# A convolution moved from VectorE to GpSimd, and 256-column mixing matmuls over two banks, in a two-layer trunk

## What is computed

```
h = RMSNorm(x);  P = h @ W_in
A  = Bg * conv3(C * xa)                      # short causal convolution, 3 taps, 512 channels
Bm = gelu(u) * (tril(W_s) LN(gelu(v)) + b)   # chunks of 128 tokens, 4 groups of 128 channels
Cm = stick-breaking attention                # 8 heads x 64, QK-norm, strictly causal
merged = sum_i sigmoid(gate_i) * (branch_i @ W_branch_out[i])
x = x + merged @ W_o
x = x + SwiGLU(RMSNorm(x)) @ W_down          # d_ff 2816
```

## Time and profile before

| | before |
|---|---|
| median of 3 runs | 1646.74 us |
| the profiled execution | 1646.1 us |
| its span | 1644.4 us |
| TensorE busy | 1636.7 us |
| VectorE busy | 969.1 us |
| ScalarE busy | 783.5 us |
| GpSimd busy | 50.8 us |
| VectorE busy in 60 to 280 us (pairs and first merge of layer 0) | 191.09 of 220 us |

### The profile page before, as it was taken

The page is one execution under the profiler, slowest core; times in us unless marked ns, Lnnn a source line. Parts: engine busy times, 40 slices in busy tenths (PEclk is TensorE's granted clock), DMA queues, the critical chain, the costliest instruction groups (busy, mean ns, idle before and its releaser), DMA issues.

```text
span 1644.4 us, 20945 instructions
## 1 busy us (share of the span) xinstructions
PE 1636.7 (100%) x7394; PEld 1360.2 (83%) x7394; DVE 969.1 (59%) x1302; ACT 783.5 (48%) x1113; POOL 50.8 (3%) x49
## 2 busy tenths in 40 slices
PE   9999999999999999999999999999999999999999
PEld 8888888888888888888888888888888888888887
DVE  6898887554554434434648888875455544344344
ACT  7788886333343223223457888763334432232231
POOL 1000000000120000000120000000001100000000
PEclk9999999999999999999999999999999999999999
DMA  5222222223323223232332222223233232323223
GB/s 195 97 68 78 78 89 72 96 89 102 102 91 101 96 96 101 90 103 89 125 119 90 77 77 77 78 77 98 94 102 102 90 102 90 102 92 99 97 95 128
DMA packets 46860, 158.15 MB, mean 96 GB/s; under 512 B 5456, under 2 KB 5712, under 8 KB 46800
## 3 DMA queue, kind: packets, MB, share of 16 engines
q1 hardware_dynamic: 46656, 157.34, 29.2%
q10 hardware_dynamic: 144, 0.03, 0.0%
HBM read 155.26 MB, written 2.10 MB: 96 GB/s over the span
## 4 chain that ended last, share of the span: by engine, by line
PE 94%; DVE 4%; ACT 1%; DVEq 1%; issue 0%; ACTq 0%
PE bank L461 28%; PE bank L462 28%; PE bank L465 28%; PE z L489 2%; PE z L563 1%; PE bank L489 1%; PE z L462 1%; PE z L465 1%; PE z L461 1%; PE misc L586 1%; PE misc L583 1%; DVE w_lo L1179 1%; PE z L552 1%; PE z L551 1%; DVE S L1348 0%; DVE v_all L1409 0%
## 5 line engine op out<-in xcount | busy, mean ns | idle before, releaser
L461 PE MATMUL bank<-xg_hi,w_hi 128*128 128x512 f32 x1472 | 574.4, 390 | 0.0
L462 PE MATMUL bank<-xg_lo,w_hi 128*128 128x512 f32 x1472 | 573.4, 390 | 0.0
L789 ACT ACTIVATE w_hi<-raw 128x1024 fp32r<-128x1024 f32 (+1 forms) x294 | 302.3, 1034 | 472.2 <-DMA raw<-in_w_units 471.8
L1179 DVE TENSOR_TENSOR w_lo<-raw,w_hi 128x1024 fp32r<-128x1024 f32 (+1 forms) x294 | 357.2, 1219 | 38.7 <-ACT w_hi L789 21.5
L465 PE MATMUL bank<-xg_hi,w_lo 128*128 128x512 f32 x1472 | 364.1, 389 | 0.0
L462 PEld LDWEIGHTS bank<-xg_lo,w_hi 128*128 128x128 f32 x1472 | 276.5, 188 | 56.9
L465 PEld LDWEIGHTS bank<-xg_hi,w_lo 128*128 128x128 f32 x1472 | 276.2, 188 | 57.2
L461 PEld LDWEIGHTS bank<-xg_hi,w_hi 128*128 128x128 f32 x1472 | 276.3, 188 | 56.8
L1184 DVE TENSOR_TENSOR S<-bank,rstd 128x512 f32<-128x512 f32 x152 | 105.0, 691 | 256.1 <-PE bank L465 254.5
L461 PE MATMUL bank<-mid_hi,w_hi 128*128 128x512 f32 x474 | 184.6, 389 | 0.0
L462 PE MATMUL bank<-mid_lo,w_hi 128*128 128x512 f32 x474 | 184.4, 389 | 0.0
(11 more groups left out here) (204 smaller groups left out, 1708.7 us busy)
## 6 DMA issues: line engine op xcount, KB each, us to landing
raw<-in_w_units SPq DMA_DIRECT2D x278, 512.0 KB, 3.3
raw<-in_w_units SPq DMA_DIRECT2D x20, 256.0 KB, 2.6
xT<-in_x SPq DMA_DIRECT2D x8, 256.0 KB, 6.4
out_x<-xT SPq DMA_DIRECT2D x7, 256.0 KB, 4.1
ln_g<-in_sgu_ln_g SPq DMA_DIRECT2D x2, 256.0 KB, 4.9
ln_b<-in_sgu_ln_b SPq DMA_DIRECT2D x2, 256.0 KB, 5.4
sgu_bias<-in_sgu_b SPq DMA_DIRECT2D x2, 256.0 KB, 5.8
sw_raw<-in_sgu_w SPq DMA_DIRECT2D x2, 256.0 KB, 6.0
```

What stands on the lines that cost most here:

```text
L461: mm(dst[:, :], wh[:, k0 + k, :], his[k], start=(k % per == 0), stop=False)
L462: mm(dst[:, :], wh[:, k0 + k, :], los[k], start=False, stop=False)
L789: af(w_hi[at.slot(c)][:, 0:kc, :], raw[at.slot(c)][:, 0:kc, :], ACT.Copy).then_inc(hi_done, 1)
L1179: tt(w[:, 0:kc, :], r[:, 0:kc, :], h[:, 0:kc, :].bitcast(F32), ALU.subtract).then_inc(lo_done, 1)
```

## The change

The five convolution instructions leave VectorE. VectorE now only signals (conv_x), and GpSimd runs the product, three scalings by a tap (tensor_scalar) and three tensor_tensor instructions more, with a drain after each. The second and third tap are a scaling into conv_part and an addition each. Two new semaphores guard the buffers: conv_read (the product has read S1 and S2, waited for before the next unit is written to S2) and mix_read.

The rounded and remainder parts of W_s lie side by side, so one matmul of 256 columns makes hi*hi and hi*lo in two halves; one of 128 columns adds lo*hi to the first half. Chunks 0 and 1 go to misc, 2 and 3 to the bank of unit 8, which unit 4 used before. VectorE adds bias and halves in four instructions of 256 columns.

The order moves: square_lo ahead of attention_lo in all pairs; in pair 0 the last LayerNorm chunk behind the causal mask; unit 4's scaling ahead of fold_sums in all pairs but the last; ya_round on ScalarE behind yb_round and the table load, ya_rest on VectorE behind the next unit 0's scaling; in the last pair the convolution starts ahead of split_lo of unit 6, and ya_round and ya_rest come after gelu_u and with_u.

```diff
+            def convolution(pairs, j):
+                tap = lambda k: par[:, R_CW + 4 * k + j:R_CW + 4 * k + j + 1]
+                pool.wait_ge(conv_x, pairs + 1)
+                nc.gpsimd.tensor_tensor(conv_in[:, 2:2 + T], S1[:, :], S2[:, :], ALU.mult).then_inc(conv_read, 1)
+                pool.drain()
+                nc.gpsimd.tensor_scalar(S1[:, :], conv_in[:, 2:2 + T], tap(2), par[:, R_CB + j:R_CB + j + 1],
+                                        ALU.mult, ALU.add)
+                pool.drain()
+                for k in (1, 0):
+                    nc.gpsimd.tensor_scalar(conv_part[:, :], conv_in[:, k:k + T], tap(k), None, ALU.mult)
+                    pool.drain()
+                    nc.gpsimd.tensor_tensor(S1[:, :], S1[:, :], conv_part[:, :], ALU.add)
+                    pool.drain()
+                nc.gpsimd.tensor_tensor(S1[:, :], S1[:, :], S0[:, :], ALU.mult).then_inc(ya_pre, 1)
                 pool.drain()
...
+                pool.wait_ge(par_in, l * 16 + 16)
+                for j in range(PAIRS):
+                    convolution(l * PAIRS + j, j)
...
-            def mix(n_misc, j, l):
+            def mix(at, n_misc, j, l):
...
+                pe.wait_ge(bank_free[at.slot(8)], at.round(8))
                 for n in range(NT):
-                    cut = slice(n * P, (n + 1) * P)
-                    mm(misc[:, cut], yb_hi[:, j, cut], sw_hi[:, j, :], start=True, stop=False)
-                    mm(misc[:, cut], yb_hi[:, j, cut], sw_lo[:, j, :], start=False, stop=False)
-                    last = mm(misc[:, cut], yb_lo[:, j, cut], sw_hi[:, j, :], start=False, stop=True)
+                    cut, base = slice(n * P, (n + 1) * P), n % 2 * 2 * P
+                    dst = misc if n < 2 else bank[at.slot(8)]
+                    mm(dst[:, base:base + 2 * P], yb_hi[:, j, cut], sw_both[:, j, :, :].rearrange("p a t -> p (a t)"),
+                       start=True, stop=False, skip_group_check=True)
+                    last = mm(dst[:, base:base + P], yb_lo[:, j, cut], sw_hi[:, j, :], start=False, stop=True,
+                              skip_group_check=True)
...
                     scores(h3 + 6, pairs + 1, 0)
+                    pe.wait_ge(mix_read, pairs + 1)
                     unit(pl["A"](j + 1), 0, xh, xl)
...
                     split_hi(at, 10)
                     yb_round()
                     ln_exp_table()
+                    ya_round()
...
+                    square_lo(l * 8 + (j * 2 + 3))
                     attention_lo(h3)
-                    square_lo(l * 8 + (j * 2 + 3))
...
                     yc_add(heads, 0)
+                    scaled(at, 4, S1[:, :])
                     fold_sums(heads + 1)
-                    scaled(at, 4, S1[:, :])
...
+                    convolution()
                     k_rest(heads + 4)
-                    convolution()
-                    mixed(m0 + M_MIX, j1)
+                    mixed(at, m0 + M_MIX, j1)
                     split_lo(at, 9)
+                    dve.wait_ge(conv_read, pairs + 1)
                     scaled(at, 6, S2[:, :])
...
-                    b = sgu_bias[:, j1, :].broadcast_to([P, NT, P])
-                    tt(N0[:, :].rearrange("p (n t) -> p n t", n=NT), misc[:, :].rearrange("p (n t) -> p n t", n=NT),
-                       b, ALU.add).then_inc(misc_free, 1)
+                    for dst, parts in halves:
+                        tt(dst, parts[:, :, 0, :], sgu_bias[:, j1, :].broadcast_to([P, 2, P]), ALU.add)
+                    dve.drain()
+                    tt(halves[0][0], halves[0][0], halves[0][1][:, :, 1, :], ALU.add).then_inc(misc_free, 1)
+                    tt(halves[1][0], halves[1][0], halves[1][1][:, :, 1, :], ALU.add).then_inc(mix_read, 1)
```

More of the change, by code:

```diff
@@ L150, in build @@
         sgu_bias = sb("sgu_bias", [P, KC, P])
-        sw_hi = sb("sw_hi", [P, KC, P], F32R)
-        sw_lo = sb("sw_lo", [P, KC, P], F32R)
+        sw_both = sb("sw_both", [P, KC, 2, P], F32R)
+        sw_hi, sw_lo = sw_both[:, :, 0, :], sw_both[:, :, 1, :]
         yb_hi = sb("yb_hi", [P, KC, T], F32R)
@@ L196, in build @@
         conv_in = sb("conv_in", [P, 2 + T])
+        conv_part = sb("conv_part", [P, T])
         N2 = conv_in[:, 2:2 + T]
@@ L289, in build @@
         yc_ok = sem("yc_ok")
+        conv_x = sem("conv_x")
+        conv_read = sem("conv_read")
         ya_pre = sem("ya_pre")
@@ L301, in build @@
         yb_bank_free = sem("yb_bank_free")
+        mix_read = sem("mix_read")
         silu_in = sem("silu_in")
@@ L1050, in pair @@
                     act.wait_ge(qk_nrm, heads + 4)
+                    if j == 0:
+                        ln_round(l, 3)
                     yc_half(m0 + M_E0)
@@ L1436, in flat @@
                         return t[:, j1, :].rearrange("p a t -> p (a t)")
-                    def tap(k):
-                        return par[:, bass.ds(j + (R_CW + 4 * k), 1)]
                     def convolution():
                         dve.drain()
[L1444 to L1452, removed]
+                        dve.sem_inc(conv_x, 1)
                     def ya_rest():
@@ L1489, in pair @@
                         split_lo(at, 7)
+                        fold_lo(heads + 1)
+                        mixed(at, m0 + M_LAST_MIX, j1)
+                        with_u(pairs)
                         ya_rest()
-                        fold_lo(heads + 1)
-                        mixed(m0 + M_LAST_MIX, j1)
-                        with_u(pairs)
                         split_lo(at, 8)
+                        dve.drain()
                         yb_rest()
@@ L1532, in pair @@
                     causal(h3 + 3)
+                    if j == 0:
+                        layer_norm(3)
                     head_norm(nch + 1, KT, par[:, R_GK:R_GK + 1])
                     softplus_sum(h3 + 3)
+                    if j == 0:
+                        layer_norm_lo(3)
                     yc_add(heads, 0)
+                    scaled(at, 4, S1[:, :])
                     fold_sums(heads + 1)
-                    scaled(at, 4, S1[:, :])
                     softplus_lo(h3 + 3)
@@ L1563, in pair @@
                     scaled(pl["A"](j + 1), 0, gates[:, KC + j + 1, :])
+                    ya_rest()
                     softplus_sum(h3 + 6)
@@ L1566, in pair, with mixed @@
                     fold_sums(heads + 2)
-                def mixed(n_misc, j1):
+                def mixed(at, n_misc, j1):
                     dve.wait_ge(misc_done, n_misc + 1)
-                    b = sgu_bias[:, j1, :].broadcast_to([P, NT, P])
-                    tt(N0[:, :].rearrange("p (n t) -> p n t", n=NT), misc[:, :].rearrange("p (n t) -> p n t", n=NT),
-                       b, ALU.add).then_inc(misc_free, 1)
+                    halves = [(N0[:, h * 2 * P:h * 2 * P + 2 * P].rearrange("p (n t) -> p n t", n=2),
+                               src[:, :].rearrange("p (n a t) -> p n a t", n=2, a=2))
+                              for h, src in enumerate((misc, bank[at.slot(8)]))]
+                    for dst, parts in halves:
+                        tt(dst, parts[:, :, 0, :], sgu_bias[:, j1, :].broadcast_to([P, 2, P]), ALU.add)
+                    dve.drain()
+                    tt(halves[0][0], halves[0][0], halves[0][1][:, :, 1, :], ALU.add).then_inc(misc_free, 1)
+                    tt(halves[1][0], halves[1][0], halves[1][1][:, :, 1, :], ALU.add).then_inc(mix_read, 1)
                 def with_u(pairs):
```

14 lines of the change are left out of this document (3 added, 11 removed).

## The result

| | before | after |
|---|---|---|
| median | 1646.67 us (1646.33 to 1647.34, 4 runs) | 1657.19 us (1656.84 to 1658.75, 4 runs) |
| the profiled execution | 1646.1 us | 1656.84 us |
| its span | 1644.4 us | 1655.1 us |

The change makes the kernel slower: ratio 1.0064, 95% interval 1.0052 to 1.0077. That is 10.5 us, where the prediction had 8.0.

What follows compares the result with a forecast made beforehand. TensorE was taken to bound the kernel (busy 1636.7 of 1644.4 us), with pairs 1 and 2 tied to VectorE. Per layer -1.6 - 2.0 + 5.0 + 0.5 + 2.1 = +4.0; 1646.1 + 8.0 + 0.6 = 1654.7 us, range 1642 to 1663.

Steps and rivals of the forecast that it cites:

- The sum: Whole kernel: gains and waits add to +4.0 us per layer, +8.0 over two layers.
- the convolution's step: Pairs: GpSimd holds VectorE 5.8 us, logs start 0.7 later, TensorE's hand-over waits total 5.0 us per layer.
- The likeliest case: Whole kernel: the forecast itself, 1654.7 us, own range 1650 to 1661, chance 0.52.
- the rival of spacing by columns: Mixing: matmul spacing follows columns, so it yields nothing, 3.3 us more, 1658; chance 0.03.
- Mixing, 0.41 each: Four mixings a layer on TensorE: 0.93 us against 1.34, gaining 1.6 per layer.
- Squares, 2.0 per layer: TensorE's wait for the squares' remainder closes: gain 1.65 us in pair 0, 0.17 in pairs 1 and 2.
- The margin of 0.4: Between VectorE's fold remainder and the cumulative matmul needing it: 0.4 us, subtracted from the first hand-over wait.
- Pair 0's mixing, 0.5: TensorE waits there for unit 4's product, whose bank the mixing takes: 0.5 us lost.
- Last mixing, 2.1: Last pair: TensorE waits for unit 4's product, 1.07 us plus up to 1.1 from GpSimd's hold; 2.1 taken.
- Heavier: Rival, GpSimd convolution: taps cost as much as products, 1.9 us more held per pair, 1663.7; chance 0.15.
- Gain: Rival, pairs: GpSimd's hold hardly occurs, no hand-over waits, -2.0 us per layer, 1642.7; chance 0.18.
- cancelled: Rival, pairs: GpSimd fits into gaps, the loop stays at 54.1 us, +0.9 per layer, 1648.5; chance 0.12.

Runs made afterwards that it cites:

- e5: Kernel before with only the squares' remainder ahead of the attention remainders and pair 0's last LayerNorm chunk behind the mask: 1646.51 us, ratio 0.9999.
- e1: Changed kernel with ya_round moved behind the fold's rounding, its remainder in the next pair: 1651.62 us, ratio 1.0029.
- e10: Kernel before with only the squares' and attention remainders exchanged, the LayerNorm chunk left in place: 1646.02 us, ratio 0.9995.
- e9: e3 with the next head's mask ahead of the weight remainder and pair 0's last LayerNorm chunk back in its old place: 1640.34 us, ratio 0.9962.
- e3: Changed kernel with ya_round behind the fold's rounding and, in the last pair, unit 4's product ahead of the fold: 1643.02 us, ratio 0.9978.
- e6: Kernel before with the new mixing alone, four reads on VectorE, unit 4's product ahead of the fold in all pairs: 1649.62 us, ratio 1.0017.
- e4: Kernel before, GpSimd also running the convolution's seven instructions on its own tiles, nobody waiting for them: 1669.25 us, ratio 1.0134.
- e7: e3 with the convolution kept on VectorE and ya_round in its old place: 1650.47 us, ratio 1.0023.

## Why the prediction was right, and where it was not

The sum said +8.0 us and the mechanism was that TensorE waits at the hand-overs of the pairs and at the last mixing. Both came out, the second in part by luck, as the convolution's step shows. The ledger of the trace: waits 7.4 + 7.0, clock 3.3, mixing -3.4, squares -4.0, together +10.3 against 10.7 of span. The likeliest case named 1654.7, the rival of spacing by columns 1658, nearer to the measured 1657.19, though what it rests on, a mixing that gains nothing, did not happen. By its steps:

- **Mixing, 0.41 each: right.** From its first matmul to the next unit's it took 0.87 us in pairs 1 and 2 and 0.94 behind the wait of pair 0 (predicted 0.93); in the last pairs, where the clock fell, 1.18 and 1.46. Before, it took 1.29 and not the 1.34 that I had put together from the steps, since the first step, from 102.67, was half as long. So 0.42 gained. The split was not as predicted: steps of 0.17 for the wide matmul and 0.06 for the narrow one behind it, instead of 0.12 and 0.112.
```profile
102.20 0.33 PE L636 MATMUL bank<-sw_both,yb_hi 128*128 128x256 f32 x1
102.37 0.22 PE L638 MATMUL bank<-sw_both,yb_lo 128*128 128x128 f32 x1
102.43 0.34 PE L636 MATMUL bank<-sw_both,yb_hi 128*128 128x256 f32 x1
```
The Trainium skill (TensorE: Matmul & The Clock Gate, Back-to-back issue gap) would have the mixing gain nothing by its gap for a single matmul, which follows the columns. The same section of the Trainium skill gives about 81 ns per 128-column matmul for a sustained stream, so it does not leave the gap to the columns alone. Here the block went from 1.29 us to 0.87: the count of matmuls mattered too.
- **Squares, 2.0 per layer: right on TensorE**, 1.65 to nothing in layer 0 (0.32 left in layer 1), and worth nothing by itself, as e5 shows. The prediction booked it as a gain and its return as a hand-over wait, which is the same sum.
- **Convolution, the price: near in its result, wrong in size and route.** This is the step that failed: "with_u ends at 164.66 + 11.0 = 175.7", and behind it "the yb rounding (0.54), a table load of 1.28 and, newly here, the ya rounding (0.53)". I priced ya_round by its 0.53 us and did not ask what it waits for. with_u in fact ended at 174.57: up to there VectorE was stretched by 1.84 us (1.14 and 0.70), not by 3.6, and by 2.8 in the whole pair, not by 5.8 (21.8 in all eight pairs). And ya_round waited 1.56 us for a convolution that took 12.6 us on GpSimd. Two errors of opposite sign: the logs start at 178.63, predicted 178.1. That the waits of 1.87, 1.20 and 0.96 came close to 2.4, 1.3 and 1.3 is luck; e1 removes most of them and leaves VectorE's stretch as it was.
- **The margin of 0.4: overrated.** Usable were 0.3 us, 0.46 less the 0.15 between the remainder's end and a waiting TensorE's start, and e5 and e10 show that the moved LayerNorm remainder had eaten 0.2 of them.
- **Pair 0's mixing, 0.5: right** (0.56 and 0.54). e9 confirms what stood in the way, the LayerNorm remainder.
- **Last mixing, 2.1: mis-sized.** The wait was 2.76: to the 1.07 that stood there already come 1.34 of fold held by GpSimd (0.40 + 0.94), where I had taken about 1.0, and 0.42 that I had not, since VectorE's softplus sums came 2.05 us later than before, TensorE only 1.63. The granted clock's fall added 1.65 per layer, a term the sum lacked altogether.
- **Rivals.** "Heavier" was half true: the taps take 1.5 us, not the 0.99 of a cheap one, but VectorE's subtraction kept its 1.22 beside one (169.50). Their length counted mostly through the queue. "Gain" and "cancelled" are excluded as stated, for the stretch is there; e3 shows that a gain of 3.65 us was within reach all the same.

## What to carry to other kernels

When work moves to another engine, follow every reader of its result in that reader's own queue: an instruction of half a microsecond costs what it waits for, and all behind it pay. How long the new engine takes counts there too, and with it what it loses to the old one. Where two engines are tied within half a microsecond, a gain on one returns as a wait at their next meeting (e5: 1.65 us gone, 1.65 back; e6: 3.4 us won on TensorE, 6.1 of new waits), so first shorten the chain that releases the meeting, here whatever starts the logs. A long wait of TensorE can be dearer than its length.

## What the runs showed of the hardware

- After idle times of up to 1.87 us in TensorE's stream the granted clock stayed at 1.00 (e.g. 135 to 139 us in the changed kernel). Around idle times of 2.56 to 2.86 us it fell in eight of nine cases (the changed kernel, e1, e4) to 0.50, that is from 2.4 to 1.2 GHz, for 3.4 us; 512-column steps then went from 0.227 to 0.427. In the changed kernel the falls began 0.65 and 0.32 us behind the restart (268.94 and 1091.56) and cost about 1.6 us each on top of the wait. In e4 they began 0.4 to 0.7 us ahead of the restart. Neither is certain: behind e4's wait of 2.86 at 968.78 there was no fall, at 1026.36 behind one of 2.85 the fall lasted 6.8 us. Nor is it the same in each execution: of e1's nine, two had a mean granted clock of 0.999 and took 1649.4 and 1649.7 us, five 0.998 and 1651.2 to 1651.9, two 0.997 and 1652.5. One fall of 3.4 us at half clock is 0.001 of the mean (estimate from the span of 1650.1). What decides it stays open. e4, a fall and a wait without one:
```profile
138.00:139.00 1.00, 0.32 (x1) 0.35 (x2) 0.97 (x2) 1.00 (x3) 0.00 (x0) 0.59 0.64 258
139.00:140.00 1.00, 1.00 (x4) 0.81 (x3) 0.95 (x2) 0.90 (x1) 0.00 (x0) 0.50 0.00 0
969.00:973.00 4.00, 4.00 (x21) 3.38 (x21) 3.94 (x5) 3.83 (x8) 0.00 (x0) 1.00 0.00 0
```
- VectorE and GpSimd hold each other: beside GpSimd the three attention remainders (L1269) took 2.32 us in pair 1, 1.62 undisturbed, and the two of k_both 2.53, undisturbed 1.39 (e7); GpSimd's tap beside the attention remainders took 2.33, undisturbed 1.57. As the Trainium skill says (GPSIMD Engine Reference, Key points), it is above all VectorE's instructions with two SBUF inputs that are held; its mixing reads from PSUM, beside two taps from 168.00 on, kept their 0.42. Two rows do not fit a simple rule: the weight remainder at 169.50, with two SBUF inputs, started beside a tap and kept its 1.22, and in e4 VectorE's own first tap, with one such tile, took 0.76 beside GpSimd's, before 0.55.
- When TensorE waited for the fold remainder, its first matmul started 0.14 to 0.15 us behind that remainder's end in every kernel here, e4 and e7 included.
- GpSimd's scaling by a tap of 512 columns took 1.53 to 1.57 us also while VectorE stood idle, but 0.99 for the first tap of pair 0. What makes the difference stays open; it wasn't tried.
